# Reordering the first attention by width, and moving modulation pieces and sums, in a two-block transformer kernel

## The reference, cut to what matters

```python
q_r = rope(q)                       # 16 heads of 64, in 2 groups of 8 heads
s = einsum(q_r, k) * scale          # k is k_s or k_w of the group
p = masked_softmax(s, kpos <= tq)
o_slc, o_win = einsum(p, v_s), einsum(p, v_w)
o = gates[0] * o_cmp + gates[1] * o_slc + gates[2] * o_win
```

## Time and profile before

| | |
|---|---|
| median of three runs | 2315.26 us (2315.2 to 2319.43) |
| the profiled execution | 2323.31 us, with a span of 2321.2 us |
| TensorE, VectorE, ScalarE, GpSimd busy | 95%, 67%, 40%, 54% of the span |
| first attention, first L1248 to the end of the last L1211 | 223.15 to 422.80 us of the span |

### The profile page before, as it was taken

One profiled execution on the slowest core, in us unless ns is written; L12 is line 12 of the kernel. 1 busy time (PEld: TensorE's weight loads), 2 busy tenths in 40 slices (PEclk: granted clock), 3 DMA queues, 4 the chain that ended last, 5 costly groups with the idle time before them and its releaser, 6 DMA issues.

```text
span 2321.2 us, 31989 instructions
## 1 busy us (share of the span) xinstructions
PE 2204.6 (95%) x11801; PEld 1970.8 (85%) x11801; DVE 1558.9 (67%) x3010; ACT 924.5 (40%) x1524; POOL 1247.5 (54%) x670
## 2 busy tenths in 40 slices
PE   4999999989998999889999999999999999999999
PEld 4887888878877788778899999999999888888887
DVE  6716767656244566544399999899993876666665
ACT  2225556432246331532233333455554333333332
POOL 0534121346431244134268888766665887878775
PEclk9989889989998999999999999999999999999999
DMA  7233333223230144024258888899998999999996
GB/s 270 91 127 129 108 101 119 91 75 100 96 104 28 50 159 146 24 76 155 73 177 292 283 276 279 279 376 338 333 359 285 365 366 359 351 348 362 350 359 225
DMA packets 164474, 492.39 MB, mean 212 GB/s; under 512 B 15072, under 2 KB 64608, under 8 KB 162912
## 3 DMA queue, kind: packets, MB, share of 16 engines
q1 hardware_dynamic: 107872, 305.79, 38.4%
q0 software_dynamic: 36864, 134.23, 15.5%
q10 hardware_dynamic: 19584, 50.34, 5.7%
HBM read 437.87 MB, written 52.43 MB: 211 GB/s over the span
## 4 chain that ended last, share of the span: by engine, by line
PE 36%; DVE 12%; POOL 1%; DMA 1%; issue 0%; ACT 0%; DVEq 0%; ACTq 0%
PE ps L2304 23%; PE ps L2268 10%; PE ps L2286 4%; DVE arena L2500 1%; DVE arena L2491 1%; DVE arena L2492 1%; DVE arena L2531 1%; DVE arena L2496 1%; DVE arena L2487 1%; DVE rope L2469 1%; DVE arena L2526 1%; DVE norm_rows L2469 1%; DVE arena L2469 1%; DVE arena L2534 1%; POOL t_split L2412 1%; DVE arena L2507 0%
## 5 line engine op out<-in xcount | busy, mean ns | idle before, releaser
L2412 POOL TENSOR_TENSOR t_split<-t_raw,t_split 128x1024 fp32r<-128x1024 f32 x225 | 549.5, 2443 | 210.5 <-ACT t_split L2338 207.6
L253 POOL TENSOR_TENSOR w_split<-ring,w_split 128x1024 fp32r<-128x1024 f32 x113 | 274.1, 2429 | 511.9 <-ACT w_split L245 500.6
L2268 PE MATMUL ps<-h_hi,t_split 128*128 128x384 f32 x2048 | 537.6, 339 | 6.4 <-POOL t_split L2412 3.4
L2304 PE MATMUL ps<-t_split,w_split 128*128 128x512 f32 x2304 | 522.9, 389 | 1.6 <-DVE w_split L2581 1.5
L2304 PEld LDWEIGHTS ps<-t_split,w_split 128*128 128x128 f32 x2304 | 432.3, 188 | 92.2 <-DVE w_split L2581 1.8
L277 PE MATMUL ps<-h_hi,w_split 128*128 128x512 f32 x1440 | 452.1, 392 | 0.0
L2338 ACT ACTIVATE t_split<-t_raw 128x1024 fp32r<-128x1024 f32 x256 | 270.3, 1057 | 337.6 <-PE ps L2304 277.4
L2268 PEld LDWEIGHTS ps<-h_hi,t_split 128*128 128x128 f32 x2048 | 373.7, 189 | 8.6 <-POOL t_split L2412 5.2
L2268 PE MATMUL ps<-h_lo,t_split 128*128 128x384 f32 x1024 | 344.1, 336 | 0.0
L277 PEld LDWEIGHTS ps<-h_hi,w_split 128*128 128x128 f32 x1440 | 270.4, 188 | 56.7 <-issue 0.7
L277 PE MATMUL ps<-h_lo,w_split 128*128 128x512 f32 x720 | 280.2, 389 | 0.0
(11 more groups left out here) (331 smaller groups left out, 3204.7 us busy)
## 6 DMA issues: line engine op xcount, KB each, us to landing
ring<-w_stream SPq DMA_DIRECT2D x219, 512.0 KB, 3.3
t_raw<-u_table SPq DMA_DIRECT2D x128, 512.0 KB
t_raw<-v_table SPq DMA_DIRECT2D x128, 512.0 KB
gelu_scratch<-e_gel ACTq DMA_DIRECT2D x128, 192.0 KB
gates_scratch<-arena ACTq DMA_DIRECT2D x8, 3072.0 KB
arena<-gelu_scratch SPq DMA_DIRECT2D x32, 768.0 KB, 5.6
arena<-gates_scratch SPq DMA_DIRECT2D x32, 768.0 KB
xT<-x_in SPq DMA_DIRECT2D x2, 1024.0 KB, 11.6
```

Source lines behind the costliest of these rows:

```text
L253: pool.tensor_tensor(w_split[:, i % RS, 1, :], ring[:, n % R, :], w_split[:, i % RS, 0, :].bitcast(F32), ALU.subtract).then_inc(lo_done, 1)
L2268: mm = pe.matmul(ps[:, 6 + n % 2, 0:NT], t_split[:, n % RAWS, u, k * P:(k + 1) * P], h_parts[h][:, k, P:T], start=(k + u + h == 0), stop=( ...
L2304: mm = pe.matmul(ps[:, 2 * i + half, :], w_split[:, b % 2, w, at:at + P], t_split[:, m % RAWS, v, half * 512:(half + 1) * 512], start=(n + ...
L2412: pool.tensor_tensor(t_split[:, m % RAWS, 1, :], t_raw[:, m % RAWS, :], t_split[:, m % RAWS, 0, :].bitcast(F32), ALU.subtract).then_inc(t_ ...
```

## The change

Widths of the 16 groups of eight units, in order: before 3 1 4 2, 3 1 4 2, 3 1 4 2, 3 1 2 4; after 4 4 3 3, 2 2 1 1, 1 1 2 2, 3 3 4 4. The two branches of a tile now stand side by side, so the query tiles are turned at other places. The 40 modulation pieces are placed behind units of width 2 to 4 alone (0.36, 0.5 and 0.6 a unit) and not near a unit of width 1; before they were spread in proportion to width. Of the five sums of this stage, two move behind the last unit of the attention (`ada_pe_last`); the sum of chunk 11 moves to the head of the expert stage. The arithmetic is the same.

```diff
@@ -814,7 +814,7 @@
         stack_hi, stack_lo, turn_hi, turn_lo = sem("stack_hi"), sem("stack_lo"), sem("turn_hi"), sem("turn_lo")
-        FIRST, NEXT, ORDER_LAST = 2, (0, 3, 1), (2, 0, 1, 3)
+        FIRST, NEXT = 3, (2, 1, 0)
@@ -1116,7 +1116,7 @@
                       act_filler=None, pool_filler=None, pe_first=None, act_first=None, dve_first=None, sink_neg=None,
-                      pe_ready=None):
+                      pe_ready=None, pe_last=None):
@@ -1212,6 +1212,8 @@
                         mm.then_inc(pv_done.sem, 1)
+                if pe_last:
+                    pe_last(pe)
@@ -1274,15 +1276,14 @@
         q_second = place("q_second", HR_AT + 2 * T, [8, P], F32R)
-        groups = [(half, branch, i) for half in range(2) for branch in range(2)
-                  for i in (ORDER_LAST if half and branch else (FIRST,) + NEXT)]
-        turns = [(0, i) for i in NEXT] + [(1, i) for i in (FIRST,) + NEXT]
+        groups = [(half, branch, i) for half in range(2) for i in ((FIRST,) + NEXT if half == 0 else range(TT))
+                  for branch in range(2)]
+        turns = [(0, i) for i in NEXT] + [(1, i) for i in range(TT)]
                 return q_first if i == FIRST else q_lower[:, :, tile_tokens(i)]
-            at = ((FIRST,) + NEXT).index(i)
-            return (q_second, q_first, q_lower[:, :, tile_tokens(NEXT[0])], q_lower[:, :, tile_tokens(NEXT[1])])[at]
+            return (q_second, q_first, q_lower[:, :, tile_tokens(NEXT[0])], q_lower[:, :, tile_tokens(NEXT[1])])[i]
@@ -1305,15 +1306,12 @@
-        TURN_AT = {1: 1, 4: 2, 18: 3, 48: 4, 56: 5, 64: 6}
-
-        def nsa_act_first(act):
-            turn_upper(act, 0)
+        TURN_AT = {1: 0, 3: 1, 6: 2, 18: 3, 28: 4, 44: 5, 60: 6}
             if n in TURN_AT:
-                if n >= 48:
-                    o_read.wait(act, n // 8 - 1)
+                if n >= 28:
+                    o_read.wait(act, 2 * (TURN_AT[n] - 3))
                 turn_upper(act, TURN_AT[n])
@@ -1347,8 +1345,8 @@
                 pool.tensor_tensor(dst, dst, gtmp[:, g % 2, :], ALU.add).then_inc(added, 1)
-                if g in (1, 4, 5, 6):
-                    t = 3 if g == 1 else g
+                if g in (1, 2, 4, 6):
+                    t = {1: 3, 2: 4, 4: 5, 6: 6}[g]
                     pool.wait_ge(added, g + 1)
@@ -1357,9 +1355,11 @@
         NSA_ADA = 5 * KD
-        ada_pace, ada_after, due = [40 * b / 310 for b in range(5)], [], 1e-6
-        for unit in nsa_units:
-            due += ada_pace[len(unit[3])]
+        ada_pace, ada_after, due = (0, 0, 0.36, 0.5, 0.6), [], 0.0
+        blocks = [len(unit[3]) for unit in nsa_units]
+        for n, b in enumerate(blocks):
+            if n >= 3 and min(blocks[n:n + 4]) >= 2:
+                due += ada_pace[b]
             ada_after.append(min(int(due), NSA_ADA))
@@ -1367,8 +1367,12 @@
+        def ada_pe_last(pe):
+            for chunk in range(3, 5):
+                ada_chunk(pe, 3 + chunk, ada_sum, 7)
+
         def ada_pe(pe, n):
-            for chunk in range(5):
+            for chunk in range(3):
                 last = (chunk + 1) * KD - 1
@@ -1376,7 +1380,7 @@
             attention("nsa", block, nsa_units, WORK, nsa_finish, nsa_finish_pool, ada_pe, ada_dve,
-                      ada_list[8 * KD - 1] + 1 + R, act_first=nsa_act_first, act_filler=nsa_act_filler, pe_ready=nsa_pe_ready)
+                      ada_list[8 * KD - 1] + 1 + R, act_filler=nsa_act_filler, pe_ready=nsa_pe_ready, pe_last=ada_pe_last)
@@ -2068,8 +2072,6 @@
                 for u in range(16, 32):
-                    if u == 16:
-                        ada_chunk(pe, 11, ada_sum12, 5)
                     left12(pe, u - 4)
@@ -2121,7 +2123,6 @@
                     out12(dve, "dve", u)
-                ada_take(dve, 11, 5)
@@ -2306,6 +2307,7 @@
+                ada_chunk(pe, 11, ada_sum12, 2)
                 pe.wait_ge(h_ready, 1)
@@ -2600,6 +2602,7 @@
                                   ALU.add).then_inc(h_ready, 1)
+                ada_take(dve, 11, 2)
                 for i in range(TT):
                 for q in range(QUADS):
```

## The result

The kernel after takes 2298.21 us (median of 7 runs, 2296.3 to 2308.94) against 2316.75 us for the kernel before (7 runs, 2310.2 to 2320.24), both measured in turn on one chip. The ratio is 0.9926 with a 95% interval of 0.9912 to 0.9941: faster by 0.7%. The profiled execution of after took 2296.3 us. That of before (2323.31) was slower than all seven of its runs here, so the traces lie 27 us apart where the medians lie 18.5 apart.

What follows compares the result with a forecast made beforehand. TensorE was taken as the bound, busy 95% of the span, with 48 us of the first attention at half clock. Terms -15.8 (attention), +1.1 (sums behind the loop), -1.2 (chunk 11) make -15.9: from 2315.26 to about 2299.5, range 2290 to 2309.

Steps and rivals of the forecast that it cites:

- Same work, 149.1 us, and the waits: First attention: scores, transposes and products stay at 149.1 us; with waits and low clock it takes 183.9 against 199.65.
- Sums, 1.84 and 3.0 for the fall, each: Attention loop: each of three remaining sums costs 1.84 us plus 3.0 for a fall of the clock, 9 in all.
- Narrow units at 0.72: 32 width-1 units: 0.72 us each at full clock, +6.1 over TensorE's floor; a fall behind unit 60 adds 4.7.
- Pieces, 6 us and part of the fill: Units of width 2 to 4: VectorE about even with TensorE at width 4, 6 us of waits elsewhere; fill about 3.5.
- Two sums behind the loop, +1.1: End of the attention: two sums, 3.7 us, plus the barrier stick out beyond the last finish by about 1.1 us.
- Chunk 11, -1.2: Its sum leaves the block of the L2081 products, -1.84 us; at the expert stage's head it costs +0.6.
- The difference carried from trace to runs: Whole kernel: the profiled execution of before, 2323.31 us, is 8 us above the median 2315.26; the same difference is assumed after.
- The first rival: Narrow stretch stays at the full clock, -4.7, and three sums cost one short fall each, some -4: 2291; chance 0.2.
- The second: Attention: waits stay at 17.4 us (+2), narrow units slow from entry (+3.6), three falls dearer (+3): 2308; chance 0.2.
- The fourth: Change comes to nothing: dearer falls after sums in widths 2 and 3, narrow stretch slow too, within 0.2%; chance 0.05.
- The third: Modulation becomes the bound: pieces of 2.2 us put 28 us more on VectorE, 2327, slower than before; chance 0.05.

Runs made afterwards that it cites:

- tiny pieces: Kernel after with pieces 2 to 8 of each chunk working on 16 of their 1024 columns, modulation not the reference's; 2292.47 us, ratio to before 0.9906.
- order_only: Kernel after with the old pacing of pieces, all five sums in the loop and chunk 11 at its old place; 2309.2 us, ratio to before 0.9968.
- pieces_spread: Kernel after with only the old pacing, pieces spread in proportion to width; 2299.93 us, ratio to before 0.9932.
- sum_in_narrow: Kernel after with the second chunk's sum at unit 50, among the narrow units, instead of unit 34; 2307.88 us, ratio to before 0.9956.

## Why the prediction was right, and where it was not

The time was forecast at 2299.5 and is 2298.21, inside the range and of the forecast sign. By its own steps:

- **Same work, 149.1 us, and the waits.** The balance held: fewer waits and less low clock, not less work. The attention is 176.1 and 176.0 us in the two traces where I had 183.9, and its mean clock 0.95 where I had 0.88 to 0.9. Two terms account for the difference of 7.8 us, and the others nearly cancel: 4.7 for a fall that didn't come, and 3.7 for the sums.
- **Sums, 1.84 and 3.0 for the fall, each.** Measured in the kernel after: 1.8, 4.6 and 4.4, that is 10.8 for three against 14.5. Two of the three falls came; the third did so in another trace (20.41 us for that group). For falls where narrow units meet wide ones I had named the group at 335.16. That was a misreading: the sum at unit 75 stands in it. The first row below has ten of that sum's sixteen instructions. The second is a group of width 1, of the kernel before, that did fall without a sum:

```profile
339.02 1.17 PE L346 MATMUL ps<-cst,ada_sum 128*128 128x1 f32 x10
...
282.95:294.92 11.97, 10.65 (x58) 10.36 (x58) 5.14 (x25) 6.23 (x25) 1.27 (x1) 0.62 0.28 90
```

- **Narrow units at 0.72.** They took 0.70. The fall behind the turn at unit 60, +4.7, did not come in either trace of after. In two other kernels a fall came 0.8 to 1.1 us behind the end of the turn, and with the turn moved two traces are even throughout. But five traces with the turn in place held the clock, and moving it made the kernel no faster. So this step of the forecast did not happen where it could be seen, and that the turn causes the falls is likely, not shown.
- **Pieces, 6 us and part of the fill.** About 8 by the tiny pieces, 2.3 of them at the fill. The forecast that VectorE reaches TensorE's pace on wide units was right. What it did not say is that this eats what the narrow units gain: with the old pacing the time is the same within the interval.
- **Two sums behind the loop, +1.1.** Measured +1.6, since they took 4.38 us and not 3.7, their second half at the lower clock.
- **Chunk 11, -1.2.** This term was mis-sized: -0.2. I took the sum as wholly on the path, -1.84; only 0.78 of it came off, since the sum had covered about 1.1 us of waiting for a copy. The other half, +0.6 on VectorE, was 0.57.
- **The difference carried from trace to runs.** The terms gave -15.9, the medians -18.5, the traces -27. The attention alone is 23.5 us shorter between the traces, 7.7 more than my terms; some 4.6 us more lie in stages that the change doesn't touch (23.5 - 1.6 + 0.2 of the 26.7 between the spans are accounted for; 1.9 of the rest stand ahead of the attention). The profiled execution of before took 6.6 us more than the median of its seven runs and that of after 1.9 less. So that the forecast lies within 2 us of the median is partly luck: terms that were 7.7 us too small against the traces met traces that lie 8.5 us further apart than the medians.

The first rival is what both traces of after show: no fall in the narrow stretch (-4.7), and sums that cost 3.7 us less in all where it had some 4, though by one fall staying out and not by three short ones. Its time, 2291, did not come, because the medians lie closer together than the traces. The second is not what they show: the waits went from 16.9 to 10.3 us of idle time. The fourth is refuted by the time. The third, slower through pieces of 2.2 us, is refuted: the 35 pieces of L338 took 1.436 us on the mean in after against 1.537:

```profile
L338 DVE SCALAR_TENSOR_TENSOR ada_sum<-ring,csil,ada_sum 128x1024 f32<-128x1024 f32 x35 | 50.3, 1436 | 0.0
```

My theory that the order alone brings the full clock fell with order_only, at 0.87. With two sums moved as well it is 0.92 (pieces_spread), and with the pieces moved too 0.95; with the old order and two sums moved it is 0.92 as well. A sum among narrow units brings the fall (sum_in_narrow); pieces there probably do, by the one fall that came behind a piece and ahead of the turn.

So the gain of 0.74% is made up of the order, 0.32%, and of two sums moved, 0.2 to 0.34%; the pieces and chunk 11 bring nothing that the runs can tell, and the small rest is within the intervals.

## What to carry to other kernels

Where the granted clock can fall behind thin work, put thin work in one place, enter it at the full clock and keep fillers and stalls out of it: behind one sum the remaining thin units cost half as much again (0.98 us against 0.65), and twice they did so behind a 1.05 us turn. A filler moved out of thin work must go somewhere, so price it at its new place too; here, in the traces, three quarters of the gain were paid back at the wider units, and the times show none of the rest. Before a small operation is counted as a gain, look at what its absence uncovers.

## What was not expected of the hardware

The granted clock fell with TensorE at 100% busy (9.22 of 9.22 us in the group with the sum) and stayed down so: 7.84 of 7.84 us at 0.50 in narrow units, two score products of 128 columns, one transpose and two products of 64 a unit; five sums of one-column products in a row ran at a mean of 0.58. The page of the Trainium skill "TensorE: Matmul & The Clock Gate", section "Why this matters for your kernels", asks for no long idle gaps; the rows of the narrow units have none, and the measurement decides: freedom from gaps was not enough here.
